# First and third mixer's norms summed on ScalarE with roots by Ln and Exp, and two position biases loaded ahead of the decay levels

## What is computed

```
for the input projection:  z = rms_norm(x) @ w_in          # 13 groups of 512 columns: mq mk mv mo hq hff hfb hi hg fu nq nk nv
y_ml = sigmoid(mo) * mLSTM(conv(mq, mk), mv, gates)         # first mixer
y_hg = head_norm(HGRN2(silu(hq), hff, hfb, hi)) * silu(hg)  # second mixer, gated decay
y_fn = real(fft2(fu))  over tokens and channels             # third mixer, "Fourier"
y_na = neighbourhood_attention(nq, nk, nv, rpb)             # fourth mixer, with position biases rpb
y    = rms_norm over each mixer's 512 columns * group_gain
h    = x + y @ w_out
```

## Time and profile before

| what | us |
|---|---|
| median of three executions | 1971.62 (1969.07 to 1973.8) |
| the profiled execution's own time | 1976.33 |
| its span, first to last instruction | 1974.4 |
| PE busy | 1836.4 (93%) |
| DVE busy | 829.5 (42%) |
| ACT busy | 520.7 (26%) |
| POOL busy | 55.3 (3%) |

### The profile page before, as it was taken

One profiled execution on the slowest core, in us unless ns is written; L12 is line 12 of the kernel. 1 busy time (PEld: TensorE's weight loads), 2 busy tenths in 40 slices (PEclk: granted clock), 3 DMA queues, 4 the chain that ended last, 5 costly groups with the idle time before them and its releaser, 6 DMA issues.

```text
span 1974.4 us, 25152 instructions
## 1 busy us (share of the span) xinstructions
PE 1836.4 (93%) x10194; PEld 1186.2 (60%) x10194; DVE 829.5 (42%) x1189; ACT 520.7 (26%) x756; POOL 55.3 (3%) x56
## 2 busy tenths in 40 slices
PE   6999999989999899999989998998989998989986
PEld 6888799889777788988754433332333332333332
DVE  3645454697654554434443332232222232232223
ACT  4444343634243444434330010010000001001002
POOL 0000000012310000000000000000000000000000
PEclk9999899989999999999989999899999899989988
DMA  7455355334465455425759999999999999999993
GB/s 269 164 170 171 128 171 165 116 126 138 131 139 148 170 181 175 150 85 202 281 240 363 398 424 427 428 429 428 428 429 422 428 430 428 428 430 428 429 429 155
DMA packets 107125, 556.73 MB, mean 282 GB/s; under 512 B 12352, under 2 KB 12584, under 8 KB 81192
## 3 DMA queue, kind: packets, MB, share of 16 engines
q1 hardware_dynamic: 97384, 427.70, 55.9%
q10 hardware_dynamic: 8640, 125.83, 15.1%
q0 software_dynamic: 1024, 2.10, 1.5%
HBM read 553.51 MB, written 2.10 MB: 281 GB/s over the span
## 4 chain that ended last, share of the span: by engine, by line
PE 76%; DMA 17%; DVE 5%; ACT 2%; issue 1%; POOL 0%; SPq 0%; DVEq 0%; ACTq 0%
PE ps L911 18%; DMA arena<-in_moe_w_dram 16%; PE ps L939 7%; PE ps L574 6%; PE ps L576 6%; PE ps L575 6%; PE ps L568 6%; PE ps L569 6%; PE ps L570 6%; PE ps L922 4%; PE ps L956 2%; PE ps L868 2%; PE ps L717 1%; DVE w_lo L1471 1%; PE ps L536 1%
## 5 line engine op out<-in xcount | busy, mean ns | idle before, releaser
L911 PE MATMUL ps<-arena 128*64 128x512 f32 x2048 | 503.1, 625 | 57.3 <-DMA arena<-in_moe_w_dram 55.6
L1471 DVE TENSOR_TENSOR w_lo<-arena,w_hi 128x1024 fp32r<-128x1024 f32 x264 | 319.2, 1252 | 289.5 <-ACT w_hi L1069 289.0
L1069 ACT ACTIVATE w_hi<-arena 128x1024 fp32r<-128x1024 f32 x264 | 264.3, 1052 | 321.6 <-PE ps L570 176.3
L911 PEld LDWEIGHTS ps<-arena 128*64 128x64 f32 x2048 | 136.3, 140 | 316.4 <-issue 247.7
L2012 DVE TENSOR_TENSOR arena<-ps,arena 128x1024 f32<-128x1024 f32 x128 | 156.6, 1225 | 234.0 <-PE ps L956 234.0
L939 PE MATMUL ps<-arena 128*64 128x512 f32 x1024 | 229.0, 600 | 0.6 <-DVE arena L1989 0.6
L939 PEld LDWEIGHTS ps<-arena 128*64 128x64 f32 x1024 | 74.3, 140 | 150.6 <-issue 148.8
L568 PE MATMUL ps<-x_hi,w_hi 128*128 128x256 f32 x512 | 147.0, 287 | 6.9 <-DVE w_lo L1471 6.9
L569 PE MATMUL ps<-x_lo,w_hi 128*128 128x256 f32 x512 | 146.2, 286 | 0.0
L570 PE MATMUL ps<-x_hi,w_lo 128*128 128x256 f32 x512 | 146.1, 285 | 0.0
L2006 DVE TENSOR_TENSOR d_lo<-ps,d_hi 128x512 fp32r<-128x512 f32 x64 | 41.3, 686 | 240.5 <-ACT d_hi L1343 240.5
(11 more groups left out here) (356 smaller groups left out, 2622.2 us busy)
## 6 DMA issues: line engine op xcount, KB each, us to landing
arena<-in_moe_w_dram SPq DMA_DIRECT2D x131, 2048.0 KB, 18.4
arena<-in_moe_w_dram ACTq DMA_DIRECT2D x60, 2048.0 KB, 14.1
arena<-in_w_in_dram SPq DMA_DIRECT2D x52, 1024.0 KB, 5.1
arena<-in_xa_wk_dram SPq DMA_DIRECT2D x16, 1024.0 KB, 5.1
arena<-in_xa_wv_dram SPq DMA_DIRECT2D x16, 1024.0 KB, 5.1
arena<-in_w_out_dram SPq DMA_DIRECT2D x16, 1024.0 KB, 5.0
arena<-in_xa_wq_dram SPq DMA_DIRECT2D x16, 1024.0 KB, 5.1
arena<-in_xa_wo_dram SPq DMA_DIRECT2D x16, 1024.0 KB, 5.1
```

The source lines that it names most:

```text
L911: last = mm(ps[rows_, m, :], xe[par][:, ECH * i + c, :], ring_up[m][i][:, c, :], start=(i == 0 and c < 2), stop=(i == ECH - 1 and c >= 2))
L1069: fn(hi_ring[(2 * n + u) % 4][:], ring_a[i][:, 2 * u:2 * u + 2, :], ACT.Copy).then_inc(S["w_hi"], 1)
L1471: V.tensor_tensor(w_lo[i][:, 2 * u:2 * u + 2, :], ring_a[i][:, 2 * u:2 * u + 2, :], hi_ring[(2 * n + u) % 4][:].bitcast(F32), ALU.subtract ...
```

## The change

The second Fourier product moves on PE from behind the last input group to behind its chunk 1, into banks 6 and 7; the third pair of the memory turn waits for its outputs. ACT and DVE copy them there, into a buffer of their own (`yfn`). ACT squares the first mixer's output with a running sum at the same place, and the third's behind the output of `nv`. DVE turns the four sums into mean squares ahead of `low` of key chunk 1. The root is `exp(-0.5 * ln(var))` on ACT, behind the Ln and the Exp of the gates, with one Newton step on DVE (`first_norms`) in level 0 of the decay, behind `low` of chunk 4; the scaling writes `y`, and the copies into `y` and both `group_norm` calls are gone. `hone` and the bias buffers get other addresses, and POOL issues the first eight bias loads once the second Fourier product is done, ahead of the levels.

```diff
@@ buffers
+        yfn, ysq = arena(164.25, NT, GW), arena(112, 4, GW)
-        hone = arena(124, T)
-        nbias = [arena(144.25, 2, T), arena(146.25, 2, T)]
+        hone = arena(188.25, T)
+        nbias = [arena(189.25, 2, T), arena(191.25, 2, T)]
@@ gpsimd
+            pool.wait_ge(S["fn_pe"], 2)
+            for m in range(2):
+                position_bias(m)
             for s in range(2 * HG_LEVELS):
...
-                if m == 0:
-                    pool.wait_ge(S["h_pe"], 2 * HG_LEVELS + 1)
-                    pool.wait_ge(S["h_mulk"], 2 * HG_LEVELS)
-                    pool.wait_ge(S["h_mulq"], 2 * HG_LEVELS)
...
+            for m in range(2, NA_H // 2 * NT):
+                pool.wait_ge(S["na_s"], m - 1)
+                position_bias(m)
@@ tensor, turn_split
+                    if n == 1 and kk == 2:
+                        pe.wait_ge(S["fn_act"], 2)
+                        pe.wait_ge(S["fn_dve"], 2)
@@ tensor, behind last_in(1)
             pe.wait_ge(S["fn_act"], 1)
             pe.wait_ge(S["fn_dve"], 1)
+            for j in range(NT):
+                for n, (tab, u) in enumerate([(0, 0), (0, 1), (1, 0), (1, 1)]):
+                    last = mm(ps[:, 6 + j, :], dft_t[:, tab, u, j * P:(j + 1) * P], fa[:, u, :, tab, :],
+                              start=(n == 0), stop=(n == 3))
+            last.then_inc(S["fn_pe"], 1)
...
             turned_split(1, NCH - 1)
-            for j in range(NT):
-                for n, (tab, u) in enumerate([(0, 0), (0, 1), (1, 0), (1, 1)]):
-                    last = mm(ps[:, 4 + j, :], dft_t[:, tab, u, j * P:(j + 1) * P], fa[:, u, :, tab, :],
-                              start=(n == 0), stop=(n == 3))
-            last.then_inc(S["fn_pe"], 1)
...
-            pe.wait_ge(S["fn_act"], 2)
-            pe.wait_ge(S["fn_dve"], 2)
@@ scalar, last input group
                     high(g, (2,))
+                    act.wait_ge(S["fn_pe"], 2)
+                    fn(yfn[:, 0, :], ps[:, 6, :], ACT.Copy).then_inc(S["fn_act"], 1)
+                    act.wait_ge(S["yv_mo"], 1)
+                    for j in range(NT):
+                        fn(ysq[:, j, :], yml[:, j, :], ACT.Square, accum_out=st[:, j:j + 1]).then_inc(S["yv_sq"], 1)
                     turned_hi(1, split["mem"][0], 3, part=range(4))
...
+            act.wait_ge(S["fn_act"], 2)
+            act.wait_ge(S["fn_dve"], 2)
+            for j in range(NT):
+                fn(ysq[:, 2 + j, :], yfn[:, j, :], ACT.Square, accum_out=st[:, 2 + j:3 + j]).then_inc(S["yv_sq"], 1)
             act.wait_ge(S["ml_y"], NH)
...
-            act.wait_ge(S["fn_pe"], 2)
-            fn(y[:, 0, 2 * GW:3 * GW], ps[:, 4, :], ACT.Copy).then_inc(S["fn_act"], 1)
+            act.wait_ge(S["yv_dve"], 1)
+            fn(st[:, 16:20], st[:, 8:12], ACT.Ln).then_inc(S["yv_ln"], 1)
             high(G_WK, (2,))
...
+            act.wait_ge(S["yv_ln"], 1)
+            fn(st[:, 24:28], st[:, 16:20], ACT.Exp, scale=-0.5).then_inc(S["yv_exp"], 1)
             high(G_WK, (3,))
-            for _ in range(2):
-                rsqrt(NT)
@@ vector
                     low(g, (2,))
+                    dve.wait_ge(S["fn_pe"], 2)
+                    V.tensor_copy(yfn[:, 1, :], ps[:, 7, :]).then_inc(S["fn_dve"], 1)
...
+            dve.wait_ge(S["yv_sq"], 4)
+            V.tensor_scalar(st[:, 8:12], st[:, 0:4], 1.0 / GW, EPS, ALU.mult, ALU.add).then_inc(S["yv_dve"], 1)
             low(G_WK, (1,))
-            dve.wait_ge(S["ts_pe"], KT)
-            step(V.tensor_copy(y[:, :, 0:GW], yml))
-            dve.wait_ge(S["fn_pe"], 2)
-            V.tensor_copy(y[:, 1, 2 * GW:3 * GW], ps[:, 5, :]).then_inc(S["fn_dve"], 1)
...
-            group_norm(0)
-            dve.wait_ge(S["fn_act"], 2)
-            dve.wait_ge(S["fn_dve"], 2)
-            dve.wait_ge(S["y_done"], 1)
-            group_norm(2)
+            def first_norms():
+                var, r, t_ = st[:, 8:12], st[:, 24:28], st[:, 32:36]
+                dve.wait_ge(S["yv_exp"], 1)
+                dve.wait_ge(S["ts_pe"], KT)
+                step(V.tensor_tensor(t_, r, r, ALU.mult))
+                step(V.scalar_tensor_tensor(t_, t_, -0.5, var, ALU.mult, ALU.mult))
+                step(V.scalar_tensor_tensor(r, t_, 1.5, r, ALU.add, ALU.mult))
+                for n, (yv, m) in enumerate(((yml, 0), (yfn, 2))):
+                    for j in range(NT):
+                        last = V.tensor_scalar(y[:, j, GW * m:GW * (m + 1)], yv[:, j, :], st[:, 24 + 2 * n + j:25 + 2 * n + j], None, ALU.mult)
+                    last.then_inc(S["y_done"], 1)
...
                 low_of(s + HG_LEAD + 1)
+                if s == 0:
+                    first_norms()
```

More of the change, by code:

```diff
@@ L303, in program @@
                   "conv_dve", "silu_act", "wg_hi", "wg_lo", "gate_pe", "gate_dve", "gate_act", "ml_pe_s", "ml_pe_m", "ml_arg",
-                  "ml_w", "ml_sw", "ml_pv", "ml_den", "ml_y", "fn_pe", "fn_act", "fn_dve",
+                  "ml_w", "ml_sw", "ml_pv", "ml_den", "ml_y", "fn_pe", "fn_act", "fn_dve", "yv_mo", "yv_sq", "yv_dve", "yv_ln", "yv_exp",
                   "hp_act", "hp_dve", "h_sub", "h_exp", "h_mulq", "h_mulk", "h_pe", "h_cp", "h_o", "h_oev",
@@ L455, in _, with position_bias @@
             nc.gpsimd.memset(buf["mv"][:, :, :, P:P + 1], 1.0).then_inc(S["pool_step"], 1)
+            rpb = ins["na_rpb"]
+            def position_bias(m):
+                i, j = m // NT, m % NT
+                for g in range(2):
+                    r = 2 * j + 1 - g
+                    for u in range(2):
+                        hd = 2 * i + u
+                        src = bass.AP(tensor=rpb.tensor, offset=rpb.offset + hd * RPB_R * RPB_C + (7 - r) * RPB_C - 48,
+                                      ap=[[1, GRID_W], [RPB_C, 4], [1, GRID_W]])
+                        pool.dma_start(nbias[m % 2][g * 64:(g + 1) * 64, u, :].rearrange("p (a w) -> p a w", w=GRID_W),
+                                       src).then_inc(S["bias_in0" if m % 2 == 0 else "bias_in1"], 16)
+            pool.wait_ge(S["fn_pe"], 2)
+            for m in range(2):
+                position_bias(m)
             for s in range(2 * HG_LEVELS):
@@ L464, in _ @@
                                         ALU.mult).then_inc(S["h_mulk"], 1)
-            rpb = ins["na_rpb"]
-            for m in range(NA_H // 2 * NT):
-                i, j = m // NT, m % NT
-                if m == 0:
-                    pool.wait_ge(S["h_pe"], 2 * HG_LEVELS + 1)
-                    pool.wait_ge(S["h_mulk"], 2 * HG_LEVELS)
-                    pool.wait_ge(S["h_mulq"], 2 * HG_LEVELS)
[L474 to L483, removed]
+            for m in range(2, NA_H // 2 * NT):
+                pool.wait_ge(S["na_s"], m - 1)
+                position_bias(m)
             def gained(n):
@@ L1616, in _ @@
                     dve.wait_ge(S["silu_act"], 3)
-                    step(V.tensor_tensor(yml, yml, buf["mo"], ALU.mult))
+                    V.tensor_tensor(yml, yml, buf["mo"], ALU.mult).then_inc(S["yv_mo"], 1)
                     dve.wait_ge(S["fn_pe"], 1)
```

## The result

The changed kernel is slower. Side by side on one chip its median is 1977.48 us (1970.05 to 1983.15, 20 executions) against 1971.41 us (1965.05 to 1976.24, 20 executions) for the kernel before: ratio 1.0035, 95% interval 1.0025 to 1.0045, that is 4.9 to 8.9 us more. The forecast had the sign and a size of 1.8 us, which lies outside this interval.

A forecast was written before the change was run, and what follows sets the result against it. PE was taken to set the time, with gaps of 7.78 us at the queries and 3.51 at the biases. Gain 0.85 less 2.65 gave 1.8 us slower: 1973.4 against the median, 1978.1 profiled; range 1966 to 1979.

The forecast's parts named there:

- Last projection chunk later by the Fourier product: On PE, the chunk ends 6.47 us later; ACT's output moves equally, its key chunk 1 step by 7.73 us.
- New waits of 2.2 and 4.7 us at key chunks 1 and 2: PE newly waits there for low parts delayed on DVE; the queries are ready before PE comes to them.
- parts 1 and 2: Moved Fourier product and norms off DVE's path: 3.0 us gained less 2.15 for low clock, 0.85 us faster.
- The norm work that moved into level 0: Reduced norm, 2.4 us on DVE behind low of chunk 4: no cost, or up to 0.5 us if cover fails.
- Part 3: Early position-bias loads: 0.27 us gained, 2.9 lost to low clock behind a 5.8 us wait; 2.65 us slower.
- 2.9 us: Low-clock cost behind block 0's softmax wait, assuming 7.8 us low: 1.08 on score products plus 1.8.
- rival 4: Clock stays low longer after the restart, some 3 us into the next dense chunk: 4.5 us slower, 1976.1; 20%.
- Rival 1: The norms' time leaves in full, PE's 7.78 us queries wait and 2.15 of low clock go: 7.3 faster; 8%.
- Rival 2: At the position-bias wait, the softmax of block 0 is not last: about 7 us faster, 1964.6; 5%.
- Rival 3: Clock stays up in all three new gaps on PE: 3.3 us faster, 1968.3; 14%.
- Rival 5: Exp and Ln share a table on ACT, chain 1.28 us earlier: 0.5 us slower, 1972.1; 3%.
- The rule on the clock: Clock recovery is paid again at every gap; speaks against making three PE gaps (2.2, 4.7, 5.8 us) of two.

The follow-up runs named there:

- e3: Changed kernel with late bias loads and the second Fourier product back behind the last input group, third mixer's squares behind both Ln: 1961.25 us against 1969.27 before.
- e2: Changed kernel with the first two position biases loaded behind the decay levels again; norms, squares and moved Fourier product stay: 1967.67 us against 1969.27 before, ratio 0.9994.
- e4: Changed kernel with 23 unused products of 128x512 in PE's wait ahead of the transposes of attention block 0: 1968.88 us against 1969.27 before, ratio 0.9994.
- e1: Kernel before with only the first eight bias loads moved ahead of the decay levels, buffers at the new address: 1975.24 us against 1969.27 before, ratio 1.0025.
- e8: Changed kernel with 11 unused products in PE's wait ahead of the transposes of attention block 0: 1973.30 us against 1969.52 before, ratio 1.0023.
- e5: Changed kernel with value chunk 4 moved into PE's wait ahead of the transposes of attention block 0: 1965.96 us against 1969.52 before, ratio 0.9974.
- e10: e4 with 19 more unused products in PE's wait ahead of key chunk 2: 1968.51 us against 1969.42 before, ratio 0.9997.

## Why the forecast was right in its steps and short in size

The range of 1966 to 1979 was met at its upper end. Its own forecasts of the mechanism ended at 4.5 us slower, and 6.07 between the medians (4.9 to 8.9 by the ratio) is more; only the 2.4 us added for scatter took it in. That the profiled execution came out at 1976.97, next to the 1978.1 forecast for it, is luck: it lies 0.5 us below its kernel's median, and the one of before, from which the 1978.1 was counted, 4.9 above.

- Last projection chunk later by the Fourier product, ACT and DVE behind it: shown. 6.86 and 8.10 us on ACT against 6.47 and 7.73; e3 undoes the move and the 7.8 us of PE's wait go.
- New waits of 2.2 and 4.7 us at key chunks 1 and 2, none at the queries: 2.2 and 4.6, none.
- Gain of parts 1 and 2, 0.85 us: 0.66 in the trace, e2 gives 0.6 in the trace and 1.2 in the times.
- The norm work that moved into level 0 costs nothing: PE's waits show none there. The early loads and their issue on POOL cost nothing by themselves: e4 keeps them and is no slower than before.
- Part 3: the scores of block 0 start 0.78 us behind the decay output, and a wait of 5.46 us (5.8 forecast) appears ahead of the transposes, ended by ACT. The transposes come 0.16 us earlier by it (0.82 less 0.66; 0.27 forecast). The mechanism holds; the mis-sized term is "2.9 us" for the low clock. It measured 6.60 us. I took the length of the low stretch from the place after 536.43 (7.8 us; by the mean of 0.79 in 544 to 545 it is 8.0), but there PE restarted with score products at a clock that was still full for 1.2 us and went into a dense chunk 3.5 us later. So the 3.54 us that I took for four score products at the low clock were partly at full clock; low throughout they take 4.55. Here PE restarts, already low, with eight transposes, a wait of 0.69, eight value products and four score products, and the dense chunk comes only after 9.1 us. That chunk was low up to 563.4, 5.7 us into it, so "some 3 us into the next dense chunk" for rival 4 was too short as well.
- Why the low stretch lasted this long was not isolated. At this place it ended 14.8, 14.1 (e1) and 11.4 us (e8) behind the restart; at key chunk 2, where dense products follow, 4.2 to 4.9 us behind it in five traces; and behind the 7.8 us wait of before, where 16 products of 128x128 come first, 4.3. So short products alone do not make it long; their small gaps, or the kind of products, may.
- Rival 4 had the right event, a low clock beyond the score products of block 1, in part 3 only (its reason, short products and waits, was not tested by itself); parts 1 and 2 did not give the -0.4 that it took. Rival 1 is false for this change and true for e3: the norms' time leaves in full once ACT isn't held back. Rival 2 is false: ACT's exponentials end last (the 2.6 us in its sum has no row behind it). Rival 3 is false: in the trace of after the clock fell at both longer waits, and in e5 and e8 behind the 2.2 us one too. Rival 5 is false: two table loads stand around the Ln in the trace of after, so the Trainium skill's rule ("ScalarE: Activation LUTs", section "Table sets") of one set for exp and ln does not describe this build.
- The rule on the clock that I set beside it ("TensorE: Matmul & The Clock Gate", section "HAM oscillation", the Trainium skill: the price is paid again at each gap) agrees with e4, e8 and e10: where the wait was filled the price was gone, where 3.0 us of it were left it was paid. It does not hold for every gap, since the 2.15 us wait brought no fall in four traces of six. Rival 4 deserved more than a fifth of the chance: the change turned a low stretch beside DVE's chain into one on PE's path.

## What to carry to other kernels

A wait that is taken away pays only up to the next thing that ends last; look what PE will stand in front of, and have work ready for it (e5), or the same edit costs time (e1). Where a low clock lies beside another engine's chain it is free (key chunk 1 in e5 and e8), and behind that chain it is paid (6.6 us here). Do not take its length from another place of the kernel: it ended 4 to 15 us behind the restart here. Before moving a product forward on PE to shorten one chain, look which chain starts behind what it pushes back.

## What the runs showed of the hardware

Products whose result nobody reads made the kernel faster: 23 of them in the wait, 6.9 us slower became 1.2 us faster. The length of a wait did not decide whether the clock fell: behind the same 2.15 us wait it fell in two traces (e5, e8) and stayed up in four (the changed kernel, e2, e4, e10). Nor was the time until it came back a constant: 4.9 us behind the restart at key chunk 2 (401.5 to 406.4), 11.4 to 14.8 us at the transposes of block 0.
